# A float32 chain of two model blocks on one core: new order at five stage borders, compression in column groups, halved last weights, and zero products in eight sparse heads

## The reference

```python
h = h + mixed                       # short convolution, then dilated attention (24 heads of 128, rotary)
h = h + squared_relu_mlp(rmsnorm(h, norm_mlp[i]), mlp_w_up[i], mlp_w_down[i])      # 4096 wide
ple_gate = jax.nn.sigmoid(rmsnorm(h, norm_ple[i]) @ ple_w_gate[i])
h = h + ple_gate * (p[i].astype(h.dtype) @ ple_w_proj[i])
...
h = h + 0.5 * _swiglu(_rmsnorm(h, ffn1_norm[layer]), ffn1_w_in[layer], ffn1_w_out[layer])   # 2816 wide
h = h + _s5_mixer(...)  or  h = h + _nsa_mixer(u, kv, w_qg[b], q_norm[b], w_o[b], rel_bias)
h = h + 0.5 * _swiglu(_rmsnorm(h, ffn2_norm[layer]), ffn2_w_in[layer], ffn2_w_out[layer])
```

## Time and profile before

| | us |
|---|---|
| three runs: median | 1822.02 |
| lowest, highest | 1820.54, 1822.83 |
| profiled execution: time | 1826.21 |
| profiled execution: span | 1824.4 |
| PE busy | 1792.2 (98%) |
| DVE busy | 1182.5 (65%) |
| ACT busy | 873.3 (48%) |
| POOL busy | 580.4 (32%) |
| mean granted TensorE clock | 0.990 |

### The profile page before, as it was taken

One profiled execution on the slowest core, in us unless ns is written; L12 is line 12 of the kernel. 1 busy time (PEld: TensorE's weight loads), 2 busy tenths in 40 slices (PEclk: granted clock), 3 DMA queues, 4 the chain that ended last, 5 costly groups with the idle time before them and its releaser, 6 DMA issues.

```text
span 1824.4 us, 35645 instructions
## 1 busy us (share of the span) xinstructions
PE 1792.2 (98%) x15466; PEld 1736.5 (95%) x15466; DVE 1182.5 (65%) x1370; ACT 873.3 (48%) x1109; POOL 580.4 (32%) x719
## 2 busy tenths in 40 slices
PE   9999999999999999999999999999999999989999
PEld 7999999999999999999998899999999998779999
DVE  7876667666674676676665966556755665756654
ACT  5354446454444544464444264444644446754442
POOL 5988870486753788000000700000000003410000
PEclk9999999999999999999999999999999998899999
DMA  7466665454444566657555345664456652025552
GB/s 278 165 229 226 225 242 182 151 193 164 156 171 151 189 219 213 221 210 311 187 201 184 122 164 210 215 237 174 162 162 217 202 187 93 24 70 183 187 195 106
DMA packets 53799, 336.59 MB, mean 184 GB/s; under 512 B 7899, under 2 KB 11020, under 8 KB 16908
## 3 DMA queue, kind: packets, MB, share of 16 engines
q1 hardware_dynamic: 46272, 300.00, 46.2%
q10 hardware_dynamic: 3276, 19.64, 2.9%
q0 software_dynamic: 4096, 14.68, 2.3%
HBM read 318.54 MB, written 15.75 MB: 183 GB/s over the span
## 4 chain that ended last, share of the span: by engine, by line
PE 89%; DVE 4%; ACT 3%; POOL 2%; DMA 1%; issue 1%; SPq 0%; ACTq 0%; POOLq 0%; DVEq 0%
PE psum L487 27%; PE psum L489 26%; PE psum L488 26%; DVE w_lo L2032 2%; ACT w_hi L1221 1%; DMA raw<-in_weights 1%; PE psum L1114 1%; PE psum L1018 1%; PE psum L1131 1%; PE psum L1112 1%; PE psum L596 1%; PE psum L831 1%; PE psum L1148 1%; PE psum L854 1%; POOL con L1992 1%
## 5 line engine op out<-in xcount | busy, mean ns | idle before, releaser
L487 PE MATMUL psum<-both,w_hi 128*128 128x256 f32 x3584 | 1005.0, 280 | 11.7 <-DVE both L2039 8.3
L488 PE MATMUL psum<-both,w_hi 128*128 128x256 f32 x3584 | 994.0, 277 | 0.0
L489 PE MATMUL psum<-both,w_lo 128*128 128x256 f32 x3584 | 994.0, 277 | 0.0
L2032 DVE TENSOR_TENSOR w_lo<-raw,w_hi 128x2048 fp32r<-128x2048 f32 x277 | 655.4, 2367 | 269.5 <-ACT w_hi L1221 268.0
L1221 ACT ACTIVATE w_hi<-raw 128x2048 fp32r<-128x2048 f32 (+1 forms) x281 | 536.3, 1909 | 538.6 <-PE psum L489 523.6
L487 PEld LDWEIGHTS psum<-both,w_hi 128*128 128x128 f32 x3584 | 675.1, 188 | 24.7 <-issue 14.6
L488 PEld LDWEIGHTS psum<-both,w_hi 128*128 128x128 f32 x3584 | 675.0, 188 | 0.5 <-issue 0.2
L489 PEld LDWEIGHTS psum<-both,w_lo 128*128 128x128 f32 x3584 | 674.1, 188 | 0.0
L1795 POOL TENSOR_TENSOR rs_tok<-var_tok,nhalf 128x2 f32<-128x2 f32 x11 | 7.8, 710 | 831.7 <-DVE var_tok L2066 831.7
L487 PE MATMUL psum<-hid_hi,w_hi 128*128 128x256 f32 x640 | 177.7, 278 | 0.5 <-ACT vcmp L1221 0.5
L488 PE MATMUL psum<-hid_lo,w_hi 128*128 128x256 f32 x640 | 176.8, 276 | 0.0
(11 more groups left out here) (393 smaller groups left out, 2029.6 us busy)
## 6 DMA issues: line engine op xcount, KB each, us to landing
raw<-in_weights SPq DMA_DIRECT2D x279, 1024.0 KB, 4.8
table<-tables ACTq DMA_DIRECT2D x8, 1792.0 KB, 8.6
tables<-st POOLq DMA_DIRECT2D x16, 512.0 KB, 4.9
tables<-st POOLq DMA_DIRECT2D x8, 256.0 KB, 5.4
tables<-turns POOLq DMA_DIRECT2D x8, 256.0 KB, 4.5
w<-in_cmp_w ACTq DMA_DIRECT2D x4, 512.0 KB, 5.4
tbl<-in_cmp_w ACTq DMA_DIRECT2D x4, 512.0 KB, 5.4
tbl<-bias_v SPq DMA_DIRECT2D x128, 16.0 KB, 4.8
```

The source lines that it names most:

```text
L487: nc.tensor.matmul(out, a_hi, b_hi, start=start, stop=False, skip_group_check=True)
L488: nc.tensor.matmul(out, a_hi, b_lo, start=False, stop=False, skip_group_check=True)
L489: return nc.tensor.matmul(out, a_lo, b_hi, start=False, stop=stop, skip_group_check=True)
L2032: tt(w_lo[:, g % RING], raw[:, g % RING], w_hi[:, g % RING].bitcast(F32), ALU.subtract).then_inc(sem["lo_ready"], 1)
```

## The change

1. Order at borders. `last_sums` splits its late weights behind all `x_low`s, no longer ahead of the last. ffn1 and ffn2 (stages with a next `x`) no longer split the unit before last inside their last pair, but there; the last unit's split stands behind `norm` of kv and of qg. At wo the third split goes behind the sums, and in mlp1 the split of wo's last slot behind the norm.
2. ple: the first square sums stand behind the fourth projection; in ple0 the next stage's first square sums stand in the middle of the last gate unit, and `norm_part` right behind ACT's last split, ahead of sine and cosine.
3. Compression: each head pair gets a 16th window of zeros (`NWIN`), so that 32 stationary columns fill a column group, and the product of token l goes to column group l mod 4. The turn becomes a plain product with a tile of four 32 x 32 identities (`ident4`), which also adds the four groups.
4. Ahead of the turns of heads 0 to 7, three products of zeros into U[0].
5. nwo: ACT and DVE split the last unit in two halves (`half_hi`, `half_lo`), and `last_unit` starts on the first. ACT makes the third and fourth square behind the splits; `square_sums(R_NWO, 0)` moves into ffn3's first unit.

```diff
--- before.py
+++ after.py
@@ -57,6 +57,8 @@
 NCMP = (SEQ - CL) // CS + 1
+NWIN = NCMP + 1
+CT = 4
 NBUCKET, MAXDIST = 32, 128
...
@@ -269,10 +271,10 @@
                 w1 = sb("w1", [P, CL, 2 * HD], scope=t)
-                blk = sb("blk", [P, CL, 2, NCMP], scope=t)
+                blk = sb("blk", [P, CL, 2, NWIN], scope=t)
                 w2 = sb("w2", [P, 2, HD], scope=t)
-                hg = sb("hg", [P, 2, 2 * NCMP], scope=t)
-                hraw = sb("hraw", [2 * NCMP, 2, P], scope=t)
+                hg = sb("hg", [P, 2, 2, NWIN], scope=t)
+                hraw = sb("hraw", [P, 2, P], scope=t)
                 posc = sb("posc", [P, 2, CL], scope=t)
@@ -545,6 +547,19 @@
 
+            def last_unit(g0, bank):
+
+                ws = slot(g0)
+                for c in range(KC):
+                    if c == 0:
+                        pe.wait_ge(sem["half_lo"], 1)
+                    if c == KC // 2:
+                        pe.wait_ge(sem["lo_ready"], g0 + 1)
+                    for m in range(2):
+                        last = exact(bank[:, m * SEQ:(m + 1) * SEQ], wide(ws, c, m),
+                                     (x_hi[0][:, c], x_lo[0][:, c]), c == 0 and m == 0, c == KC - 1)
+                last.then_inc(sem["unit_done"], 1)
+
             def token_unit(g0, k, x, bank, mid=None):
@@ -690,7 +705,7 @@
                 up_unit(g, 0, x, A_BANK, (sem["xl_ready"], XBASE[r], 1), fin_last if fin else None,
-                        squares=(n, 2) if normed and not fin else None)
+                        squares=(n, 0 if f == 3 else 2) if normed and not fin else None)
                 if side is not None:
@@ -731,21 +746,19 @@
                         pe.wait_ge(sem["h_ready"], hbase(n) + m)
-                    if m == 3:
-                        square_sums(n, 0)
                     for q in range(2):
...
                 last.then_inc(sem["unit_done"], 1)
+                square_sums(n, 0)
                 for m in range(PAIRS):
...
                         pe.wait_ge(sem["gate_scaled"], PAIRS * l + 1)
-                    if m == 3 and l == 0:
-                        square_sums(R_PLE0, 0)
                     up_unit(g + 1 + m, 0, XBUF[n], GB[l][m], (sem["xl_ready"], XBASE[n], 1) if m == 0 else None,
-                            (lambda: norm_bcast(n)) if m == 1 else None,
+                            (lambda: norm_bcast(n)) if m == 1 else (lambda: square_sums(R_PLE0, 0))
+                            if m == 3 and l == 0 else None,
                             head=(lambda: norm_sum(n)) if m == 1 else None, squares=(n, 2) if m == 0 else None)
@@ -1015,25 +1028,26 @@
                         rows = slice(half * HD, (half + 1) * HD)
-                        last = nc.tensor.matmul(DB[half][0:2 * NCMP, 0:P],
+                        part = slice(l % CT * 2 * NWIN, (l % CT + 1) * 2 * NWIN)
+                        last = nc.tensor.matmul(DB[half][part, 0:P],
                                                 blk[rows, l, :, :].rearrange("p c n -> p (c n)"),
                                                 [w1, w1v][kind][rows, l, :],
-                                                start=l == 0, stop=l == CL - 1, skip_group_check=True)
+                                                start=l < CT, stop=l >= CL - CT, skip_group_check=True)
                         if l == CL - 1:
...
                 for half in range(2):
-                    last = nc.tensor.transpose(DB[0][:, half * 2 * NCMP:(half + 1) * 2 * NCMP],
-                                               hraw[:, half, :], ident[0:2 * NCMP, 0:2 * NCMP])
+                    last = nc.tensor.matmul(DB[0][:, half * 2 * NWIN:(half + 1) * 2 * NWIN], hraw[:, half, :],
+                                            cst("ident4", 2 * NWIN), start=True, stop=True, skip_group_check=True)
                 last.then_inc(sem["hid_turned"], 1)
...
                     rows = slice(half * HD, (half + 1) * HD)
-                    last = nc.tensor.matmul(DB[3][rows, 0:2 * NCMP], w2[:, 0, :], hg[:, half, :],
+                    last = nc.tensor.matmul(DB[3][rows, 0:2 * NCMP], w2[:, 0, :], hg[:, half, :, 0:NCMP],
                                             start=True, stop=True, skip_group_check=True)
...
@@ -1124,6 +1138,8 @@
                     pe.wait_ge(sem["n_ta"], hd)
+                if hd < NH // 2:
+                    keep_warm(3, U[0])
                 pe.wait_ge(sem["n_near"], hd + 1)
@@ -1211,8 +1227,7 @@
             third_part(KC - 1)
-            square_sums(R_NWO, 0)
-            up_unit(g + 3, 0, 0, DB[1])
+            last_unit(g + 3, DB[1])
             ffn(3, R_NWO)
@@ -1409,6 +1424,8 @@
                 split(g + 4)
+                if r != R_FIN:
+                    norm_part(r)
 
@@ -1552,7 +1569,6 @@
 
-            norm_part(R_PLE0)
             norm(R_PLE0)
@@ -1666,14 +1682,14 @@
                 for half in range(2):
-                    last = copy(hraw[:, half], DB[half][0:2 * NCMP, 0:P])
+                    last = copy(hraw[:, half], DB[half][:, 0:P])
                 last.then_inc(sem["hid_copied"], 1)
...
                     act.wait_ge(sem["w2_done"], 1)
-                act_fn(hg[:].rearrange("p e n -> p (e n)"), DB[0][:, 0:4 * NCMP],
+                act_fn(hg[:].rearrange("p e a n -> p (e a n)"), DB[0][:, 0:4 * NWIN],
                        ACT.Gelu_apprx_tanh).then_inc(sem["hg_ready"], 1)
@@ -1761,12 +1777,20 @@
             g = BASE["nwo"]
-            split(g)
+            s, half = g % RING, UNIT // 2
+            done(g)
+            act.wait_ge(raw_landed[s], 16 * ((g + RING) // RING + 1))
+            copy(w_hi[:, s, 0:half], raw[:, s, 0:half]).then_inc(sem["half_hi"], 1)
+            copy(w_hi[:, s, half:], raw[:, s, half:]).then_inc(sem["hi_ready"], 1)
             for m in range(PAIRS):
-                residual(R_NWO, m)
+                act.wait_ge(sem["h_ready"], hbase(R_NWO) + m + 1)
+                x_high(R_NWO, m)
                 if m < 2:
+                    squares(R_NWO, m)
                     split(g + 1 + m)
             split(g + PAIRS - 1)
+            for m in range(2, PAIRS):
+                squares(R_NWO, m)
             ffn(3, R_FFN3, R_NWO)
@@ -2088,10 +2112,10 @@
                         add(m, two(banks[m]), scale)
-                    if m == PAIRS and late is not None:
-                        split(late)
                     if m and x:
                         x_low(r, m - 1)
+                if late is not None:
+                    split(late)
 
@@ -2132,8 +2156,11 @@
 
-                split(late)
+                if l == 0:
+                    split(late)
                 norm(n)
+                if l:
+                    split(late)
                 split(g)
@@ -2217,12 +2244,10 @@
                 for k in range(0, FFN_PAIRS - 1):
-                    pair(k, f == 0 and k == FFN_PAIRS - 2)
+                    pair(k, k == FFN_PAIRS - 2)
                 if f == 0:
                     dve.wait_ge(sem["h_ready"], hbase(r))
-                last_sums(g + 3 * FFN_PAIRS - 1, r, 0.5, x)
-                if f:
-                    split(g + 3 * FFN_PAIRS - 1)
+                last_sums(g + 3 * FFN_PAIRS - 1, r, 0.5, x, late=g + 3 * FFN_PAIRS - 2 if x else None)
 
@@ -2470,8 +2495,9 @@
                     attend(HEAD_PAIRS - 1, at)
-                split(BASE["wo"] + m)
-            last_sums(BASE["wo"] + PAIRS - 1, R_WO, 1.0, True, WO)
+                if m < PAIRS - 2:
+                    split(BASE["wo"] + m)
+            last_sums(BASE["wo"] + PAIRS - 1, R_WO, 1.0, True, WO, late=BASE["wo"] + PAIRS - 2)
 
@@ -2559,6 +2585,7 @@
             norm(R_FFN1)
+            split(BASE["ffn1"] + 3 * FFN_PAIRS - 1)
             dve.wait_ge(sem["rs_ready"], R_FFN1 + 1)
@@ -2566,10 +2593,12 @@
                     dve.wait_ge(sem["hid_done"], 2)
+                if kind == 0:
+                    dve.memset(blk[:, :, :, NCMP], 0.0)
                 for a in range(2):
...
                     windows = bass.AP(whole.tensor, whole.offset, [list(whole.ap[0]), [CS, NCMP], [1, CL]])
-                    last = tt(blk[:, :, a, :].rearrange("p l n -> p n l"), windows,
+                    last = tt(blk[:, :, a, 0:NCMP].rearrange("p l n -> p n l"), windows,
                               posc[:, kind].unsqueeze(1).broadcast_to([P, NCMP, CL]), ALU.add)
@@ -2632,6 +2661,7 @@
             norm(R_FFN2)
+            split(BASE["ffn2"] + 3 * FFN_PAIRS - 1)
             ts(qe[:], var_tok[:], EPS / NSCALE ** 2, None, ALU.mult).then_inc(sem["q_var"], 1)
@@ -2727,7 +2757,13 @@
                 add(m, two(DB[2 + m]))
-            split(g)
+            s, half = g % RING, UNIT // 2
+            dve.wait_ge(sem["half_hi"], 1)
+            tt(w_lo[:, s, 0:half], raw[:, s, 0:half], w_hi[:, s, 0:half].bitcast(F32),
+               ALU.subtract).then_inc(sem["half_lo"], 1)
+            dve.wait_ge(sem["hi_ready"], g + RING + 1)
+            tt(w_lo[:, s, half:], raw[:, s, half:], w_hi[:, s, half:].bitcast(F32),
```

(5 more changed lines are left out.)

## The result

| | before | after |
|---|---|---|
| median of the runs, us | 1828.05 (20 runs) | 1814.59 (20 runs) |
| lowest, highest | 1818.09, 1835.42 | 1799.89, 1823.72 |
| ratio, 95% interval | | 0.9931 (0.991 to 0.9953) |
| profiled execution: time, span | 1826.21, 1824.4 | 1817.22, 1815.3 |
| mean granted clock | 0.990 | 0.996 |

The change saves 0.7%, 12.6 us by the ratio, where 21.7 were forecast (1800.3 us). Both kernels spread over more than 17 us from run to run, and the three runs shown beforehand lay low in that spread: their median was 1822.0, that of 20 runs is 1828.05. So of the 14.3 us between the forecast time and the measured one, 6.0 come from the base and the rest from the gain.

What follows compares the result with a forecast made beforehand. TensorE (PE), busy in every slice, was taken to bound the kernel. 4.2 + 2.0 + 7.6 + 5.7 + 2.2 = 21.7 us off the 1822.0 us median gave 1800.3 us (54%), range 1794 to 1810.

Steps and rivals of the forecast that it cites:

- Part 1: Borders ffn1 to kv, ffn2 to qg, wo to mlp1: PE starts earlier; 4.2 us gained, bounds 0 to 4.8.
- Part 2: ple0 to qkv: waits for a square and for ACT's copy of partial sums go; 2.0 us gained, bounds 0.8 to 2.3.
- The other move: First square sums behind the fourth projection: two squares come 1.7 us later, hidden by a unit.
- Part 3: Both compression runs (L1018) get shorter in column groups, the first capped by ACT's copies; 7.6 us gained, bounds -0.4 to 8.6.
- Part 4: Heads: products of zeros keep the clock up; 5.7 us gained, bounds 8.9 gained to 10.2 lost.
- Part 5: nwo's last unit starts earlier on halved weights, partly lost to waits in ffn3; 2.2 us gained, bounds 0 to 5.
- The step that decided: Between stage borders PE takes a 256-column matmul each 0.113 us, 5.43 per unit; DVE and ACT work there costs nothing.
- (a): Rival: all gains land fully, no half clock in the heads, eight compression tiles at once; 1796 us, chance 15%.
- (b): Rival: column groups take turns, so the compression change gains nothing and its turns cost 0.4 us; 1808 us, chance 8%.
- (d): Rival: the moved `w_lo` splits at the borders come late, twice 2.3 us; 1805 us, chance 8%.
- (e): Rival: slower than before, zeros keep the whole stretch of heads at half clock; 1836.8 us, chance 3%.
- (c): Rival: the clock in the heads falls as often as before, so the zeros gain 0; 1806 us, chance 12%.

Runs made afterwards that it cites:

- e8: Changed kernel with the weight splits of ffn1's and ffn2's last unit but one put back inside their last pair: 1818.0 us in one run.
- e1: The changed kernel run again without an edit: 1810.7 us, ratio 0.9916.
- e3: Changed kernel with ACT issuing the positions' transfer ahead of mlp0's third and fourth square, and mlp1's first table turn one pair later: 1803.8 us, ratio 0.9878.
- e5: Kernel of e3 without the three products of zeros ahead of the turns of heads 0 to 7: 1811.2 us, ratio 0.9913.
- e6: Kernel of e3 with the first turn of the compressed keys moved into the middle of ffn2's second unit: 1805.9 us, ratio 0.9882.
- e7: Kernel of e6 with the products of zeros in heads 0 to 3 only: 1803.7 us, ratio 0.9868.
- e15: Kernel of e6 run again unchanged, as base for other runs: 1805.8 us, ratio 0.9879.

## Why the prediction was wrong

The measured terms, at one pace, are the lengths of the stretches around each place in two profiles of each kernel:

| stretch | before | after | gained | forecast |
|---|---|---|---|---|
| ple0's sum to qkv's sum | 27.42, 27.40 | 26.55, 27.13 | 0.6 | 2.0 |
| late qkv to mlp1's sum | 64.50, 64.48 | 63.51, 63.49 | 1.0 | 1.0 |
| mlp1's sum to ple1's sum | 188.68, 188.72 | 190.31, 190.31 | -1.6 | 0 |
| late ffn1 to kv's sum | 47.24, 47.23 | 45.56, 45.55 | 1.7 | 1.6 |
| kv's sum into ffn2 | 85.89, 85.89 | 78.95, 77.32 | 7.8 | 7.6 |
| late ffn2 to qg's sum | 44.51, 44.51 | 42.82, 42.82 | 1.7 | 1.6 |
| qg's sum to ffn3's sum | 135.93, 129.57 | 127.65, 124.77 | 6.5 | 7.9 |

**Part 1** was right at its borders, and e8 gives both of the 1.6 us back when it is undone. (Its upper bound adds up to 4.9 us, not 4.8.) What failed is its step "There two splits now follow the norm; the third unit's has 0.9 us to spare": it counted PE's units and DVE's relu, and left out POOL, which makes mlp1's table in the same stretch. First POOL in the kernel before, its norm step and the table's last product:

```profile
603.44 0.72 POOL L1795 TENSOR_TENSOR rs_tok<-var_tok,nhalf 128x2 f32<-128x2 f32 x1 [40.23 <-DVE var_tok L2066]
...
632.04 0.46 POOL L1898 TENSOR_TENSOR st<-pw 128x128 f32<-128x128 f32 x1
```

Then the kernel after, the same norm step and POOL with DVE's `w_lo` ahead of the turn:

```profile
600.98 0.72 POOL L1819 TENSOR_TENSOR rs_tok<-var_tok,nhalf 128x2 f32<-128x2 f32 x1 [39.23 <-DVE var_tok L2090]
...
629.85 0.46 POOL L1922 TENSOR_TENSOR st<-pw 128x128 f32<-128x128 f32 x1
630.31 2.29 DVE L2056 TENSOR_TENSOR w_lo<-raw,w_hi 128x2048 fp32r<-128x2048 f32 x1 [0.75 <-ACT w_hi L1236]
...
630.39 2.69 POOL L1919 TENSOR_TENSOR pw<-st,a 128x256 f32<-128x256 f32 x1
633.04 0.61 POOL L1920 TENSOR_TENSOR pw<-st,a 128x256 f32<-128x256 f32 x1
...
634.14 0.46 POOL L1922 TENSOR_TENSOR st<-pw 128x128 f32<-128x128 f32 x1
...
634.65 1.09 PE L648 MATMUL psum<-con,ab 128*128 128x128 f32 x8 [1.41 <-POOL st L1922]
```

The product that takes 0.61 us alone takes 2.69 where DVE's `w_lo` of 2.29 runs beside it. The Trainium skill (SBUF — State Buffer, SBUF: two separate sides) says that DVE and GpSimd share a port pair under an exclusive lock held for the whole instruction; these rows agree. Before, POOL went from its norm step to the table's last product in 29.1 us, five of its products held up in this way, and ended 3.0 us ahead of PE's turn at 635.54. After, seven are held up, it takes 33.6 us and ends 2.1 later, and PE comes 2.5 us sooner.

**Part 2** was right on the waits it named, both are gone, and wrong in "The other move, the first square sums behind the fourth projection, delays two squares by 1.7 us behind a unit that hides them". Behind those squares stands an issue on ACT's queue, the positions. DVE in the kernel after:

```profile
304.33 0.29 DVE L2266 CAST ang<-posi 128x256 f32<-128x256 int32 x1 [2.55 <-DMA posi<-in_positions]
...
305.71 0.16 DVE L2090 TENSOR_SCALAR var_tok<-psum 128x2 f32<-128x2 f32 x1
...
307.19 0.70 PE L626 MATMUL psum<-diag,ones 128*128 128x256 f32 x2 [1.05 <-DVE diag L2094]
```

DVE waits 2.55 us for them and makes the norm's variance behind that; PE waits 1.05 for the diagonal (1.5 in e1). In the kernel before, DVE began the same cast at 301.31 without a wait. With the issue ahead of the squares (e3) the stretch is 25.23 us: 2.2 gained, and 2.0 were forecast.

**Part 3** was right in size and in kind. A run of the compression takes 2.03 us (1.75 to 3.5 forecast) and the first is capped by ACT's copies, by 1.46 us. At full clock (e1) it gave 8.6. The rule of the Trainium skill that the prediction weighed (TensorE: Matmul & The Clock Gate, Part 3: Packing small matmuls), no overlap within a row group, would have left 7.2 us; these rows go against it. The same section of the Trainium skill has three column tiles at 2.38 times the speed, and with that these rows agree in kind: four groups took 2.03 us instead of 7.18.

**Part 4** had the mechanism, and e5 shows it. Its size was off: of the last row's 6.5 us part 5 has 2.8, so 3.7 are left for it, where 5.7 were forecast. The forecast came from one execution with 27.3 us at half clock; the second had 10.2. The clock of the runs gives about the same (an estimate): 30 us at half before and 13 after are 17 less, and at half clock the products of zeros followed each other in 427 ns instead of 216, so that is worth at most half, 8.6 us, less 5.2 for the zeros. (24 products at half clock are 10.4 us, not 10.2.) The prediction also weighed what the Trainium skill (TensorE: Matmul & The Clock Gate, Part 4: PE-mode transpose) says of transposes; on that no run decides: e5 and e6 have the same turns.

**Part 5** was right: 20.61 and 20.47 us from the last matmul of nwo's third unit to ffn3's sum before, 17.71 and 17.70 after, with the three waits where they were expected, 1.2, 1.5 and 0.8 us. 2.8 gained, 2.2 forecast.

**The step that decided** stands ahead of the parts: "PE takes one 256-column matmul each 0.113 us", with the conclusion that nothing between the borders costs time. A 256-column matmul has two paces, and the earlier trace rows show only one. The terms above with the rest of the kernel make 18.5 us at one pace (1809.9 as the mean of two profiles, 1791.4 after). The slow pace took some of it back: 11.6 us on average in two profiles of before, 19.0 in the two of after. That leaves 11 us, against 12.6 and 15.3 by the ratios; with two profiles of each kernel it is an estimate. What part of it the change itself brings is known for one stage only, and from profiles: with the wait ahead of the table turn mlp1 was slow behind it in four of five, without it in none of twelve. ffn1 was slow from its start in 3 of 17, all three with the change (the first profile, e5, e7), but neither e1 nor the two profiles of before; whether the change makes it more frequent is open. mlp0 was slow in two (e8, e15), though e15 is the kernel of e6 unchanged, which was fast there. Had both waits been seen, the sum would have been some 19 us, still 3 to 6 more than the ratios give.

Rivals (a), (b), (d) and (e) did not come; of (c) only that the clock without zeros differs from run to run. None of them held a second pace.

## What to carry to other kernels

When a border is reordered, list what else stands in each of the moved instruction's queues, issues of transfers too, and look at POOL wherever a DVE instruction on two SBUF tensors is moved next to it. Before a time is forecast from one profile, count matmuls per 100 us stage by stage and see whether the stages agree: here one part in 25 hid between them at a granted clock of 1.00, and it differs from run to run. To compare two kernels whose runs spread by 1%, compare the lengths of single stretches and not the totals: at one pace and full clock most of those above repeat within 0.04 us.

## What the runs showed of the hardware

- A stream of 256-column f32 matmuls with a new stationary operand each goes at 113.3 or 117.8 ns from start to start, both at a granted clock of 1.00, and keeps its pace for up to 1511 matmuls. The interruptions set it: the same group of foreign products without a wait ahead of it nearly always turns it the same way, and a wait leaves it open. The norm's four narrow sums are followed by 117.8 ns; the table's eight turns (128 of 131 cases in the 17 profiles) and its sixteen narrow products (136 of 136) turn either pace into the other. What in PE holds the state no run here shows. The Trainium skill (TensorE: Matmul & The Clock Gate, Wait — 56ns, not 53.3ns?) gives columns over 2.4 GHz and 2.5 ns more, by which an estimate for 256 is 109.2 ns; neither pace is that.
- Column groups of one row group overlap: 128 products of 64 rows, 32 stationary columns and 128 moving ones in 2.03 us, 16 ns each, where 7.18 us were needed in two tiles.
